# Joining the three TensorE pieces of an attention step, with a bank of its own for the weighed values and a pause of the steps around the second reload of the sums

## The reference, cut to what matters

```python
h = x * (1.0 + scale) + shift
proj = h @ w_in[layer] + b_in[layer]                  # 2048 x 1024 times 1024 x 8704
# attention, 3 groups of 4 heads, dilation 1, 4, 16, blocks of 128 queries:
scores = einsum('..qhd,..khd->..hqk', qs, kb) * dh ** -0.5 + alibi     # window of 1 or 2 blocks of keys
m = scores.max(-1); p = exp(scores - m); den = p.sum(-1)
out = einsum('..hqk,..khd->..qhd', p / den, vb)
mix_w = softmax(stack(lses), axis=0)                  # weights of the 3 groups
y_attn = (sum_g mix_w * out_g * silu(z_attn)) @ w_proj_attn[layer]
y_conv = (g_b * conv3(g_c * u_x) * silu(z_conv)) @ w_proj_conv[layer]
merged = sigmoid(g_mix_a) * y_attn + sigmoid(g_mix_b) * y_conv
x = layer_norm(alpha * x + gate * (merged @ w_out[layer] + b_out[layer]))
```

## Time and profile before

| | |
|---|---|
| median of 3 runs (lowest, highest) | 2014.13 us (2011.61, 2014.8) |
| profiled execution: its own time | 2009.24 us |
| its span, from first to last instruction | 2007.5 us |
| PE busy | 1920.3 us, 96% |
| PE weight loads busy | 1517.8 us, 76% |
| DVE busy | 1228.4 us, 61% |
| ACT busy | 857.6 us, 43% |
| granted TensorE clock, mean | 0.989 |

### The profile page before, as it was taken

One profiled execution on the slowest core, in us unless ns is written; L12 is line 12 of the kernel. 1 busy time (PEld: TensorE's weight loads), 2 busy tenths in 40 slices (PEclk: granted clock), 3 DMA queues, 4 the chain that ended last, 5 costly groups with the idle time before them and its releaser, 6 DMA issues. The chain is left out here.

```text
span 2007.5 us, 25472 instructions
## 1 busy us (share of the span) xinstructions
PE 1920.3 (96%) x8989; PEld 1517.8 (76%) x8989; DVE 1228.4 (61%) x2168; ACT 857.6 (43%) x1512; POOL 201.1 (10%) x356
## 2 busy tenths in 40 slices
PE   3799999999999999999998999999999999999996
PEld 3588888777777777777776777778887878887885
DVE  5655564445666666655666666667657565556775
ACT  2544453444455445466676544444344510012221
POOL 0022211111000000011211000000011100000000
PEclk9899999999999999999998999999999999999998
DMA  8566743343222232255764232223245688883441
GB/s 311 194 194 188 231 163 113 111 110 90 79 76 78 79 90 82 73 167 161 256 218 164 72 95 79 81 74 76 85 153 158 206 218 226 239 288 123 142 144 74
DMA packets 303645, 289.03 MB, mean 144 GB/s; under 512 B 38340, under 2 KB 255552, under 8 KB 299808
## 3 DMA queue, kind: packets, MB, share of 16 engines
q1 hardware_dynamic: 277280, 199.01, 34.3%
q0 software_dynamic: 26240, 88.40, 12.3%
HBM read 198.97 MB, written 88.38 MB: 143 GB/s over the span
## 5 line engine op out<-in xcount | busy, mean ns | idle before, releaser
L1018 PE MATMUL acc<-t_hi,w_hi 128*128 128x512 f32 x1904 | 771.9, 405 | 19.2 <-ACT room L1195 8.0
L1020 PE MATMUL acc<-t_lo,w_hi 128*128 128x512 f32 x1904 | 747.2, 392 | 0.0
L1021 PE MATMUL acc<-t_hi,w_lo 128*128 128x512 f32 x1904 | 745.6, 392 | 0.0
L1018 PEld LDWEIGHTS acc<-t_hi,w_hi 128*128 128x128 f32 x1904 | 358.8, 188 | 131.3 <-issue 49.7
L1021 PEld LDWEIGHTS acc<-t_hi,w_lo 128*128 128x128 f32 x1904 | 359.0, 189 | 79.3
L1020 PEld LDWEIGHTS acc<-t_lo,w_hi 128*128 128x128 f32 x1904 | 359.4, 189 | 68.2 <-issue 0.2
L1430 DVE TENSOR_TENSOR room<-acc,part 128x512 f32<-128x512 f32 x204 | 140.8, 690 | 224.8 <-PE acc L1021 223.1
L1234 ACT ACTIVATE part<-acc,cols 128x512 f32<-128x512 f32 x204 | 140.2, 687 | 244.3 <-PE acc L1021 244.0
L1430 DVE TENSOR_TENSOR room<-room 128x512 f32<-128x512 f32 (+3 forms) x222 | 178.3, 807 | 92.3 <-DMA room<-wg_d 41.8
L1216 ACT CAST w_hi<-w_raw 128x512 fp32r<-128x512 f32 x272 | 167.6, 616 | 97.8 <-PE acc L1021 95.7
L1430 DVE TENSOR_TENSOR w_lo<-w_raw,w_hi 128x512 fp32r<-128x512 f32 x272 | 184.2, 685 | 29.6 <-ACT w_hi L1216 29.5
(11 more groups left out here) (204 smaller groups left out, 2072.7 us busy)
## 6 DMA issues: line engine op xcount, KB each, us to landing
w_raw<-in_w_in SPq DMA_DIRECT2D x136, 512.0 KB, 5.2
gate_d<-room POOLq DMA_DIRECT2D x64, 256.0 KB, 2.7
w_raw<-gate_d SPq DMA_DIRECT2D x32, 512.0 KB, 5.2
qk_d<-room POOLq DMA_DIRECT2D x24, 512.0 KB, 4.3
room<-qk_d SPq DMA_DIRECT2D x192, 64.0 KB, 2.7
ada_w<-in_w_ada SPq DMA_DIRECT2D x8, 1024.0 KB, 11.9
room<-in_x SPq DMA_DIRECT2D x32, 256.0 KB, 6.1
t_raw<-tr_d SPq DMA_DIRECT2D x8, 1024.0 KB, 8.2
```

Source lines behind the costliest of these rows:

```text
L1018: nc.tensor.matmul(to, w_hi[:, s, k], t_hi[:, p, k], start=(first and k == 0), stop=False, skip_group_check=True)
L1020: nc.tensor.matmul(to, w_hi[:, s, k], t_lo[:, p, k], start=False, stop=False, skip_group_check=True)
L1021: mm = nc.tensor.matmul(to, w_lo[:, s, k], t_hi[:, p, k], start=False, stop=(last and k == KH - 1), skip_group_check=True)
```

## The change

The three PE pieces of attention stand together, once per step: `weigh_values(k-2)`, `turn_probs(k-1)`, `scores(k)` behind the same product, so weighing comes a slot later than before. The weighed values go into the first quarter of `xb` (`o_ps`); the transposes now wait for `pt_ready` (the copy of the last probabilities) and weighing waits for `o_ready`. The slots are a list, `ATT_AT`: one per 3 slots from 119 (before 93), none in slots 298 to 312, so it ends at 424 (before 383). The gate sums are two pieces at slots 265 and 268. `turn_stats` moves from slot 385 to 426, `weigh_groups` from round 397 to 436, `mix` from rounds 446 and 456 to 452 and 462, and the loads, scalings and stores of the output matrix by 4 slots.

```diff
-ATT0 = FIRST[1] + 4 * NP + 2
+ATT0 = FIRST[1] + 8 * NP
 NSTEP = NPAIR * NBLK
-ATT_END = ATT0 + 3 * NSTEP
-STAT = ATT_END + 4
+PAUSE = (FIRST[2] - 3, FIRST[2] + 12)
+ATT_AT = []
+for k in range(NSTEP + 2):
+    slot = ATT_AT[-1] + 3 if k else ATT0
+    ATT_AT.append(PAUSE[1] if PAUSE[0] <= slot < PAUSE[1] else slot)
+ATT_END = ATT_AT[-1]
+STAT = ATT_END + 2
 BG2 = G_GATE0 * NP + 1
-WEIGH = STAT + 12
+SUM_AT = [at + 2 for at in ATT_AT if at >= BG2 + 16][:2]
+WEIGH = STAT + 10
-MIX_AT = (NS - 30, NS - 20)
+MIX_AT = (NS - 24, NS - 14)
...
+        o_ps = xb[:, 0:P]
...
                 def turn_probs(k):
                     pe.wait_ge(exp_done, k + 1)
                     if k:
-                        pe.wait_ge(o_ready, k)
+                        pe.wait_ge(pt_ready, k)
...
                 def weigh_values(k):
                     pe.wait_ge(pt_ready, k + 1)
+                    if ATT_AT[k + 2] > SUM_AT[0]:
+                        pe.wait_ge(gbc_done, sum(ATT_AT[k + 2] > at for at in SUM_AT))
+                    if k == 0:
+                        pe.wait_ge(v_copied, 4 * len(VG))
+                    else:
+                        pe.wait_ge(o_ready, k)
                     pe.wait_ge(att_in[k % 2], 48 * (k // 2 + 1))
...
-                                mm = nc.tensor.matmul(po[cols_h, 0:P], v_ring[:, step % 4, cols_h],
+                                mm = nc.tensor.matmul(o_ps[cols_h], v_ring[:, step % 4, cols_h],
...
                 def turn_stats():
-                    pe.wait_ge(max_ready, NSTEP)
-                    pe.wait_ge(exp_done, NSTEP)
+                    pe.wait_ge(o_ready, NSTEP)
...
-                    k, r = divmod(n - ATT0, 3)
-                    if r == 0 and 0 <= k - 1 < NSTEP:
-                        turn_probs(k - 1)
-                    if r == 0 and 0 <= k < NSTEP:
-                        scores(k)
-                    if r == 2 and 0 <= k - 1 < NSTEP:
-                        weigh_values(k - 1)
-                    if n == BG2 + 18:
-                        sum_gate()
+                    if n in ATT_AT:
+                        k = ATT_AT.index(n)
+                        if k >= 2:
+                            weigh_values(k - 2)
+                        if 1 <= k <= NSTEP:
+                            turn_probs(k - 1)
+                        if k < NSTEP:
+                            scores(k)
+                    for half in range(2):
+                        if n == SUM_AT[half]:
+                            sum_gate(half)
...
-                    if r == 0 and 0 <= k < NSTEP:
-                        bias_max(k)
-                    if r == 2 and 0 <= k - 1 < NSTEP:
-                        take_o(k - 1)
+                    if m - 1 in ATT_AT[:NSTEP]:
+                        bias_max(ATT_AT.index(m - 1))
+                    if m - 2 in ATT_AT[2:]:
+                        take_o(ATT_AT.index(m - 2) - 2)
```

More of the change, by code:

```diff
@@ L740, in _ @@
                                 load_t(ph, p)
[L741 to L743 removed]
+                    if m + 2 in ATT_AT[:NSTEP]:
+                        load_att(ATT_AT.index(m + 2))
                     for k in range(KT + 1):
@@ L1067, in turn_probs, with weighed @@
                     tr.then_inc(turned, 1)
+                def weighed(slot):
+                    return sum(at <= slot for at in ATT_AT[2:])
                 def weigh_values(k):
                     pe.wait_ge(pt_ready, k + 1)
+                    if ATT_AT[k + 2] > SUM_AT[0]:
[4 more added lines that the diff above has]
+                        pe.wait_ge(o_ready, k)
                     pe.wait_ge(att_in[k % 2], 48 * (k // 2 + 1))
@@ L1077, in weigh_values, with sum_gate @@
                                 step = k if half == k % 2 else k - 1
-                                mm = nc.tensor.matmul(po[cols_h, 0:P], v_ring[:, step % 4, cols_h],
+                                mm = nc.tensor.matmul(o_ps[cols_h], v_ring[:, step % 4, cols_h],
                                                       prob_t[:, h, half * P:(half + 1) * P], start=(half == 0), stop=(half == 1))
                         else:
-                            mm = nc.tensor.matmul(po[cols_h, 0:P], v_ring[:, k % 4, cols_h], prob_t[:, h, 0:P],
+                            mm = nc.tensor.matmul(o_ps[cols_h], v_ring[:, k % 4, cols_h], prob_t[:, h, 0:P],
                                                   start=True, stop=True)
                     mm.then_inc(pv_done, 1)
-                def sum_gate():
+                def sum_gate(half):
                     pe.wait_ge(gacc, KT)
-                    for half in range(2):
-                        if half:
-                            pe.wait_ge(gbc_done, 1)
-                        nc.tensor.matmul(xb[:], ones[:], gate_acc[:, half * CH:(half + 1) * CH],
-                                         start=True, stop=True).then_inc(gsum, 1)
+                    if half:
+                        pe.wait_ge(gbc_done, 1)
+                    pe.wait_ge(o_ready, weighed(SUM_AT[half]))
+                    nc.tensor.matmul(xb[:], ones[:], gate_acc[:, half * CH:(half + 1) * CH],
+                                     start=True, stop=True).then_inc(gsum, 1)
                 def turn_stats():
-                    pe.wait_ge(max_ready, NSTEP)
-                    pe.wait_ge(exp_done, NSTEP)
+                    pe.wait_ge(o_ready, NSTEP)
                     for w, a in enumerate((all_m, all_d)):
@@ L1348, in _ @@
                             za_sigmoid(g, 3)
-                    k, r = divmod(m - 1 - ATT0, 3)
-                    if r == 1 and 0 <= k < NSTEP:
-                        soften(k)
-                    if r == 0 and 0 <= k - 1 < NSTEP:
-                        copy_probs(k - 1)
+                    if m - 2 in ATT_AT[:NSTEP]:
+                        soften(ATT_AT.index(m - 2))
+                    if m - 1 in ATT_AT[1:NSTEP + 1]:
+                        copy_probs(ATT_AT.index(m - 1) - 1)
                     if m < 5:
@@ L1845, in _ @@
                             gate_row(k)
-                        if m == BG2 + 22 + 2 * k + 2:
+                        if m == BG2 + 26 + 2 * k + 2:
                             scale_wo(k)
-                    if m == BG2 + 19:
-                        gate_sum(0)
-                        gate_sum(1)
+                    for half in range(2):
+                        if m == SUM_AT[half] + 1:
+                            gate_sum(half)
                     if m == STAT + 1:
```

17 lines of the change are left out of this document (6 added, 11 removed).

## The result

The changed kernel takes **1988.3 us** (median of 4 runs, 1988.07 to 1988.75); the kernel before took 2014.47 us in the runs beside it. The ratio is 0.9881, 95% interval [0.9866, 0.9895], so 26 us are gone by the two medians and 24 by the ratio, where I forecast 30.4. The time lies in the range and on the side that held 0.94, and 4 us above the likeliest value. But two terms of the sum that looked like one number are not what I took them for, as the experiments show.

The account below looks back on a forecast made before the run. PE, busy 96% of the span, was taken as the bound. Terms of 9.3 + 11.9 + 12.2 + 1.1 - 0.2 - 3.9 = 30.4 us came off the 2014.13 us median, giving 1984 us, range 1974 to 1996.

Parts of the forecast that it names:

- join: In the attention steps on PE: one restart fewer saves 0.11 us (two blocks) or 0.08 (one) per step, 9.3 us in all.
- own bank, the wait gone: At the transposes: the wait for the copy of weighed values moves to the next weighing, saving 11.9 us outside the reload.
- pause: At the second reload: no steps in slots 297 to 312, so 1.5 us of 13.7 us excess stays, saving 12.2 us.
- mix(0): At slot 454: PE stands 3.9 us for a take behind the mixing, then the clock falls; 3.9 us more lost than before.
- Rival A: At the joined steps: the four shape changes stay and the join saves nothing, 1993 us; chance 0.16.
- So the reload work alone hides.: Step for the second reload, argued from the first: 7 products there, without attention, take 19.5 us against 19.04 bare.
- if the reload keeps a wait of ScalarE for the gate stores: At the reload: one of the signs named as showing the forecast wrong, with no size given.
- sign of some 44.5 us for the 14 products: At the reload: the 14 products would take about 44.5 us, at a clock of 1.0.
- Rival B: At the reload: it stays slow from rounding, gate and za rounds; only 4.6 us of transposes' waits go, 1992 us; chance 0.14.
- Gate sums: Between the two gate sums: PE's wait of 1.31 us (1.47 with the hidden part) goes for one more restart, saving 1.1 us.
- rival C: At the join and mix(0): first load hidden (15 us for 9.3), mix costs 0.5 for 3.9, 1975 us; chance 0.1.
- The difference between profile and median: Whole kernel: the median lies 4.9 us above the profiled 2009.24 us, so the saving was taken off the median, 2014.13 us.

## Why the prediction was right, and where not

Taken apart by the runs, each beside the one that differs in one thing (gains in us; a ratio's difference is taken of 2012 us):

| term | forecast | measured: medians | by the ratios | by the starts |
|---|---|---|---|---|
| join | 9.3 | 12.1 | 11.7 | 9.8 |
| own bank, the wait gone | 11.9 | 7.9 | 9.9 | 11.1 |
| pause (three pairs) | 12.2 | 0.7, -2.3, 0.8 | 0.4, -2.0, 1.6 | -1.2, -2.2, 0.0 |
| first step 26 slots later | no term | 7.6 | 7.0 | 4.3 |
| mix(0) (two pairs) | -3.9 | -4.3, -4.4 | -4.2, -4.0 | -5.0, -6.4 (slots 428 to 474) |

The runs also make one chain from the kernel before to the changed one: 2012.4 us, 2004.8 with the first step 26 slots later, 2008.9 with the gate sums and the mixing moved as well (the bank is there, but the old wait is kept), 2008.2 with the pause, 2000.4 with the wait gone, 1988.3 with the join. These are the 24 us of the ratio, so no part of the change is left over.

That the time came out near the forecast is in part luck: 12.2 us for the pause are worth nothing, and the 7.0 to 7.6 us of the shift, which I had no term for, and some more from the join stand in their place.

*The join*: right. The rows of the joined step are those forecast to 0.01 us, and a clean step saves 0.15 us (two blocks) or 0.07 (one) where I had 0.11 and 0.08. Rival A falls with the run that undoes the join. The Trainium skill, TensorEngine Tiling (Array Packing), Key Properties, has TensorE drained at each change of tiling mode. The rows agree that each change costs a pause (0.32 instead of 0.23 us in front of weighing), and the number of changes did stay the same; but what stands behind a change isn't of one price. A restart of the products costs 0.11 in the first matmul and 0.13 to 0.17 in the whole product, a first load ahead of the transposes 0.06, and the join trades one for the other.

*The moved wait*: right as a mechanism, and a little over-sized. No wait of L1071 for the copy is left. The term took the waits of before, 14.9 us, as if they stayed the same under the new offset of the steps; put back there, they are 9.2 us in all, the reload's included, or 11.0 with the hidden 0.16 each, which is what the starts give for the whole term (11.1).

*The pause*: wrong, and this is the step of the prediction that failed: "So the reload work alone hides." I argued from the first reload, which hides entirely, that without steps the second would too. But the second one stands in gate groups, with a sigmoid on ScalarE that waits for a store, and beside the 1 MB loads of the reload that store lands after 6.3 to 6.6 us and not 3.2. I had named it among the signs ("if the reload keeps a wait of ScalarE for the gate stores") and gave it no price. It could have been read before the change: ScalarE waits there for 6.34 us in the reload, and PE's wait of 2.06 us for ScalarE at 1067.38 comes 5 us behind it, with ScalarE at work all the time in between but for 0.17 us:

```profile
1062.58 0.69 ACT L1243 ACTIVATE room<-acc,cols 128x512 f32<-128x512 f32 x1 [6.34 <-DMA gate_d<-room]
```

With that wait taken away the excess falls from 7.9 to 3.5 us; those 3.5 are left with the pause and without it, and their rows are takes behind splits of the sums (1.68 us). What makes them late I have not taken apart further. My sign of some 44.5 us for the 14 products was wrong in itself as well, as it held steps that the pause carries off: bare products and 1.5 us would have been 39.6; measured are 46.0. Rival B had this mechanism half: the reload stays slow. It gave the remaining gain to the waits of the transposes, 4.6 us, and 1992 us in all.

*What came in its place*: the shift of the first step, a line of the diff that I read as a plain delay. Alone it gives 7.6 us, more than half of what I had put to the pause. By the starts it is 4.3 us, 3.8 of it at the reload (8.6 us of excess for 12.4), where the idles that the steps' waits add up to are followed by the low clock once and not twice. The other 3.3 us of the median I put to the clock of the executions that aren't profiled (0.989 to 0.991 with the shift, 0.986 to 0.991 before); that is argued from the list of runs, and no trace shows it.

*Gate sums*: forecast 1.1 us. Slots 263 to 269 have 6.7 us of excess in the run with the wait and no pause, and 8.3 with 26 slots alone, 1.6 less; the steps there differ a little too.

*mix(0)*: right in place, cause and idle (3.9 us forecast, 3.71 and 0.16 hidden measured). The clock cost 2.7 us instead of 1.7. So rival C falls, which needed a mix without a bite and a first load that is hidden (0.06 us of it are in view).

*The difference between profile and median*: I took it off unchanged. It was 4.9 us before and is 0.2 after. This helped: in the profiles the gain is 21.1 us.

## What to carry to other kernels

- Where pieces of work are woven in at a fixed period among groups of another period, a shift of the start is an edit with a price of its own: one slot was worth 10 us here. Try the shifts one by one, and do so before crediting a gain to what came along with the shift.
- Before giving work a rest around a busy stretch, look for what holds the busy stretch up by itself: the wait that starts the chain was on another engine and 20 us ahead of PE's idle (5.65 us of ScalarE for a store), and one buffer gave 7.5 us where the pause gave none.
- Long work on VectorE (6.3 us of mixing here) has a right place inside a group: behind the last take, not ahead of one. Three rounds later or four earlier was worth 4 us, and later cost 1.3 us again at the next consumer.

## What the runs showed of the hardware

- A single idle's length did not tell in these traces whether TensorE's clock falls behind it. Behind idles of PE of 3.47 us and more, past the first 90 us, the level of 1.2 GHz came each time (ten idles, eight of them the 3.71 or 3.72 us at mix(0)). In the middle range it went either way: it came behind 1.56 us (the buffer without the pause), 1.95 us and 2.55 us, and it did not behind 1.79 us and, in the kernel before at 872 us, 2.60 us. The wait of 2.64 or 2.65 us ahead of L1192 (L1175 before the change) stands in all 14 traces, and the low level came at it in 8 of them. Where it came, it cost 1.5 to 3.3 us beside the idle: the wait of 2.55 us costs 4.4 in all.
- A store of 256 KB landed after 3.2 us in a quiet stretch of gate groups and after 6.3 to 6.6 us around loads of 1 MB.
- The spread of one kernel's executions goes with its mean clock: 2006.42 us at 0.990 and 2014.31 us at 0.986. This is what can set a profiled execution 5 us from the median, and it is why every term above is given by medians and by the starts.
